# Seven quarter-block products in place of eight in the up projections of the two gated layers

## The reference

```python
D_MODEL = 1024
SEQ = 512
D_FF = 2816

def swiglu(x, w_in, w_out):
    gate, up = jnp.split(x @ w_in, 2, axis=-1)
    return (jax.nn.silu(gate) * up) @ w_out

h = h + 0.5 * swiglu(rmsnorm(h, ffn1_norm[l]), ffn1_w_in[l], ffn1_w_out[l])
h = h + hybrid_mixer(rmsnorm(h, mix_norm[l]), ...)
h = h + 0.5 * swiglu(rmsnorm(h, ffn2_norm[l]), ffn2_w_in[l], ffn2_w_out[l])
```

## Time and profile before

| | |
|---|---|
| median of 3 runs | 2323.24 us |
| profiled execution, whole | 2322.17 us |
| its span, first to last instruction | 2320.4 us |
| TensorE busy | 2283.2 us (98%), 13952 matmuls |
| TensorE weight loads busy | 1889.1 us (81%) |
| VectorE busy | 1155.9 us (50%) |
| ScalarE busy | 913.2 us (39%) |
| GpSimd busy | 1149.5 us (50%) |
| mean granted TensorE clock | 0.994 |

### The profile page before, as it was taken

How to read it: one execution, slowest core, us unless ns; L and a number is a source line. 1 busy time by engine, 2 the same in 40 slices (tenths; PEclk the granted TensorE clock), 3 DMA queues, 4 the chain that set the end, 5 groups by cost and what they waited for, 6 DMA issues and landing times.

```text
span 2320.4 us, 36943 instructions
## 1 busy us (share of the span) xinstructions
PE 2283.2 (98%) x13952; PEld 1889.1 (81%) x13952; DVE 1155.9 (50%) x1772; ACT 913.2 (39%) x1456; POOL 1149.5 (50%) x687
## 2 busy tenths in 40 slices
PE   8999999999999999999999999999999989999998
PEld 7888887889988888877777778888888878888887
DVE  5442146268743431377545466614626986731732
ACT  5332225467753321255644274212234535222222
POOL 5444444544465554444555354444445973544442
PEclk9999999999999999999999999999999989999999
DMA  4232233320033322331111113223222232332231
GB/s 167 99 99 92 99 99 102 122 69 1 10 100 100 98 93 98 98 120 64 47 34 53 43 56 104 93 97 99 93 97 84 92 100 82 100 99 99 91 99 55
DMA packets 56126, 200.09 MB, mean 86 GB/s; under 512 B 6224, under 2 KB 6480, under 8 KB 56016
## 3 DMA queue, kind: packets, MB, share of 16 engines
q1 hardware_dynamic: 54432, 195.82, 25.7%
q10 hardware_dynamic: 1584, 2.75, 0.4%
HBM read 196.45 MB, written 2.10 MB: 86 GB/s over the span
## 4 chain that ended last, share of the span: by engine, by line
PE 44%; POOL 4%; issue 3%; DVE 2%; ACT 1%; POOLq 0%; DVEq 0%; ACTq 0%
PE ps L133 13%; PE ps L135 13%; PE ps L134 13%; POOL sb_w_lo L114 2%; POOL sb_caway L3060 1%; PE ps L647 1%; PE ps L2068 0%; DVE ps L3111 0%; PE ps L661 0%; POOL sb_cu_lo L3072 0%; POOL sb_cout L3066 0%; PE ps L2064 0%; PE ps L2115 0%; PE ps L2044 0%; PE ps L2013 0%
## 5 line engine op out<-in xcount | busy, mean ns | idle before, releaser
L114 POOL TENSOR_TENSOR sb_w_lo<-sb_w_raw,sb_w_hi 128x1024 fp32r<-128x1024 f32 (+1 forms) x361 | 887.1, 2460 | 929.9 <-ACT sb_w_hi L101 928.4
L133 PE MATMUL ps<-sb_xn_hi,sb_w_hi 128*128 128x512 f32 x1688 | 669.5, 397 | 6.2 <-POOL sb_w_lo L114 3.2
L134 PE MATMUL ps<-sb_xn_lo,sb_w_hi 128*128 128x512 f32 x1688 | 657.9, 390 | 0.0
L135 PE MATMUL ps<-sb_xn_hi,sb_w_lo 128*128 128x512 f32 x1688 | 657.9, 390 | 0.0
L101 ACT ACTIVATE sb_w_hi<-sb_w_raw 128x1024 fp32r<-128x1024 f32 x362 | 379.8, 1055 | 484.1 <-PE ps L135 458.1
L133 PEld LDWEIGHTS ps<-sb_xn_hi,sb_w_hi 128*128 128x128 f32 x1688 | 316.6, 188 | 78.5 <-POOL sb_w_lo L114 4.0
L135 PEld LDWEIGHTS ps<-sb_xn_hi,sb_w_lo 128*128 128x128 f32 x1688 | 316.5, 188 | 67.2
L134 PEld LDWEIGHTS ps<-sb_xn_lo,sb_w_hi 128*128 128x128 f32 x1688 | 316.6, 188 | 65.9 <-issue 2.2
L133 PE MATMUL ps<-sb_hid_hi,sb_w_hi 128*128 128x512 f32 x864 | 336.4, 389 | 2.0 <-DVE sb_hid_lo L401 2.0
L135 PE MATMUL ps<-sb_hid_hi,sb_w_lo 128*128 128x512 f32 x864 | 336.1, 389 | 0.0
L134 PE MATMUL ps<-sb_hid_lo,sb_w_hi 128*128 128x512 f32 x864 | 336.1, 389 | 0.0
(11 more groups left out here) (491 smaller groups left out, 2957.1 us busy)
## 6 DMA issues: line engine op xcount, KB each, us to landing
sb_w_raw<-weights SPq DMA_DIRECT2D x365, 512.0 KB, 3.4
sb_stage<-x SPq DMA_DIRECT2D x4, 512.0 KB, 4.7
out<-sb_out_stage SPq DMA_DIRECT2D x8, 256.0 KB, 2.9
sb_abias<-table ACTq DMA_DIRECT2D x4, 256.0 KB, 5.4
sb_lora_w<-lora ACTq DMA_DIRECT2D x2, 256.0 KB, 2.8
sb_rstd<-table ACTq DMA_DIRECT2D x1, 256.0 KB, 2.7
sb_root<-table ACTq DMA_DIRECT2D x1, 256.0 KB, 3.0
sb_ss<-table ACTq DMA_DIRECT2D x1, 256.0 KB, 3.4
```

What stands on the lines that cost most here:

```text
L114: pool.tensor_tensor(c.w_lo[:, slot, 0:width], c.w_raw[:, slot, 0:width], c.w_hi[:, slot, 0:width].bitcast(F32), ALU.subtract).then_inc(c. ...
L133: pe.matmul(out, hi, rhs_hi(k0 + k), start=first, stop=False)
L134: pe.matmul(out, hi, rhs_lo(k0 + k), start=False, stop=False)
L135: mm = pe.matmul(out, lo, rhs_hi(k0 + k), start=False, stop=last)
```

## The change

In 38 of the 44 pairs of the gated layers (pairs 2 to 15 of each `upA`, pairs 1 to 5 of each `upB`), the gate tile and the up tile are no longer computed as two units of 8 k-tiles x 512 tokens. The pair is treated as a 2 x 2 block matrix times a 2 x 2 block matrix: the weights are A11, A12 (gate columns, lower and upper half of the 1024 features), A21, A22 (up columns), each 4 k-tiles; the activations are two feature halves by two token halves of 256. Winograd's form of Strassen's method then needs seven products of quarter blocks: each is 4 k-tiles x 3 passes = 12 matmuls of 256 columns, so a pair is 84 matmuls of 256 columns in place of 48 of 512.

What it takes around the products:

- Four weight sums for each pair, S1 = A21+A22, S2 = S1-A11, S3 = A11-A21, S4 = A12-S2 (`block_sum`, VectorE, 128x512 each, read from `w_raw`), each split into hi (`block_high`, ScalarE) and lo (`block_low`, VectorE).
- Four activation sums T1 to T4, once for each layer (`fold_x_dve`, `fold_x_act`), for four k-tiles; they are made before pair 0 is evacuated.
- Seven additions of products in PSUM, in six instructions for each pair (`fold_adds`, VectorE), and one copy (`fold_copy`, ScalarE).
- The high part of the hidden tile moves from VectorE (L399 before) to ScalarE (`parts` in `fold_up_act`).
- GpSimd splits only the gate unit (128x1024) and A22 (128x512), and the gate unit only once VectorE has finished the pair's four sums.
- The loops of these stages are written out. `c.gate` now lies in `c.y`. Some semaphores are shared to make room for new ones.

The core of the diff. TensorE:

```diff
+def fold_up_pe(pe, c, phase, xn_ready, first, i):
...
+    def folded(p):
...
+        pe.wait_ge(c.s_lo, p.u + 1)
+        pe.wait_ge(c.s_evac, p.u + START - 2)
+        block_products(pe, c, p1, p.first.spots[0], *x_part(0, 0), True, True).then_inc(c.s_used, 1)
+        block_products(pe, c, p2, p.first.spots[1], *x_part(HALF_K, 0), True, True).then_inc(c.s_used, 1)
+        pe.wait_ge(c.s_block_lo, phase.t.low + 2 * HALF_K)
+        pe.wait_ge(c.s_block_lo, p.low["S2"])
+        block_products(pe, c, p6, p.spot["S2"], *t_part(2), True, True).then_inc(c.s_used, 1)
+        pe.wait_ge(c.s_block_lo, p.low["S1"])
+        block_products(pe, c, p5, p.spot["S1"], *t_part(0), True, True).then_inc(c.s_used, 1)
+        pe.wait_ge(c.s_block_lo, p.low["S3"])
+        block_products(pe, c, p7, p.spot["S3"], *t_part(1), True, True).then_inc(c.s_used, 1)
+        pe.wait_ge(c.s_block_lo, p.low["S4"])
+        block_products(pe, c, p3, p.spot["S4"], *x_part(HALF_K, HALF_T), True, True).then_inc(c.s_used, 1)
+        pe.wait_ge(c.s_lo, p.u + 2)
+        block_products(pe, c, p4, p.spot["A22"], *t_part(3), True, True).then_inc(c.s_pe, 2)
...
+            if p.j == 1 and phase.prepared:
+                pe.wait_ge(c.s_rs, i + 1)
```

ScalarE's and VectorE's order in a pair (`after` is the next pair):

```diff
+def fold_up_act(act, c, phase, gated, hid_base, i):
...
+    for j, p in enumerate(pairs):
+        after = pairs[j + 1] if j + 1 < len(pairs) else None
+        if p.folded:
+            block_high(act, c, p, "A22")
+        if j > 0:
+            parts(pairs[j - 1])
+        if p.folded:
+            fold_copy(act, c, phase, p)
+        unit_high(act, c, after.first if after is not None else phase.following[0])
+        if after is not None and after.folded:
+            block_high(act, c, after, "S2")
+            block_high(act, c, after, "S1")
...
+        if j == 0 and phase.prepared:
+            fold_x_act(act, c, phase, i)
+        activations(p)
+        if after is not None and after.folded:
+            block_high(act, c, after, "S3")
+            block_high(act, c, after, "S4")
...
+def fold_up_dve(dve, c, phase, gated, hid_base, gain, i):
...
+        if j > 0:
+            hidden(pairs[j - 1])
+        if j > 0:
+            low(pairs[j - 1])
+        if j == 0 and phase.prepared:
+            fold_x_dve(dve, c, phase, gain, i)
+        if after is not None:
+            block_sum(dve, c, after, "S1")
+            block_sum(dve, c, after, "S2")
+            block_sum(dve, c, after, "S3")
+        if p.folded:
+            fold_adds(dve, c, p, 0)
+        if after is not None:
+            block_low(dve, c, after, "S2")
+            block_low(dve, c, after, "S1")
+            block_sum(dve, c, after, "S4")
+        if p.folded:
+            fold_adds(dve, c, p, 1)
+            fold_adds(dve, c, p, 2)
+        if gated:
+            gate = result(c, phase, p, 0)
...
+            dve.tensor_tensor(gate, gate, shaped(p, c.rs[:]), ALU.mult).then_inc(c.s_gated, 1)
+        if after is not None:
+            block_low(dve, c, after, "S3")
+            block_low(dve, c, after, "S4")
...
```

The additions, the waits of ScalarE's copies on TensorE, and GpSimd's part:

```diff
+def fold_adds(dve, c, p, n):
...
+    if n == 0:
+        dve.wait_ge(c.s_copied, p.copied)
+        dve.wait_ge(c.s_used, p.used["S2"])
+        dve.tensor_tensor(right, p6, left, ALU.add).then_inc(c.s_add, 1)
+        dve.tensor_tensor(p2, p2, left, ALU.add).then_inc(c.s_add, 1)
+    elif n == 1:
+        dve.wait_ge(c.s_used, p.used["S3"])
+        dve.wait_ge(c.s_add, p.add + 2)
+        dve.tensor_tensor(left, p7, right, ALU.add).then_inc(c.s_add, 1)
+        dve.tensor_tensor(right, p5, right, ALU.add).then_inc(c.s_add, 1)
+        dve.wait_ge(c.s_add, p.add + 3)
+        dve.tensor_tensor(p5, p5, left, ALU.add).then_inc(c.s_add, 1)
+    else:
+        both = c.ps[:, folded_banks(p.j)[1]]
+        dve.wait_ge(c.s_pe, p.u + START + 2)
+        dve.wait_ge(c.s_add, p.add + 5)
+        dve.tensor_tensor(both, both, c.ss[:], ALU.add).then_inc(c.s_add, 1)
...
+def fold_low(pool, c, phase, between=None):
...
+        if p.folded:
+            low = c.lo_blocks[:, p.spot["A22"]]
+            pool.wait_ge(c.s_hi, p.u + 2)
+            pool.tensor_tensor(low, c.w_raw[:, (p.u + 1) % RING, HALF_K:], c.hi_blocks[:, p.spot["A22"]].bitcast(F32),
+                               ALU.subtract).then_inc(c.s_lo, 1)
+        if after is not None:
+            if after.folded:
+                pool.wait_ge(c.s_sums, after.sums + 4)
+            unit_low(pool, c, after.first)
```

The activation sums, for each of four k-tiles (t1, t3 lie in `rstd`, t2, t4 in `ss`):

```diff
+        dve.tensor_scalar(product, c.x[:, k], gain(k), None, ALU.mult).then_inc(c.s_sums, 1)
...
+        dve.tensor_tensor(t1, product[:, HALF_T:], product[:, 0:HALF_T], ALU.subtract).then_inc(c.s_sums, 1)
+        dve.scalar_tensor_tensor(out=t3, in0=other[:, HALF_T:], scalar=g, in1=product[:, HALF_T:], op0=ALU.mult,
+                                 op1=ALU.subtract).then_inc(c.s_sums, 1)
...
+        dve.scalar_tensor_tensor(out=t2, in0=other[:, HALF_T:], scalar=g, in1=t1, op0=ALU.mult,
...
+        dve.scalar_tensor_tensor(out=t4, in0=other[:, 0:HALF_T], scalar=g, in1=t2, op0=ALU.mult,
...
+        for x, source in enumerate((c.rstd, c.ss)):
...
+            dve.tensor_tensor(c.t_lo[:, 2 * x:2 * x + 2, k], halves(source[:]),
+                              c.t_hi[:, 2 * x:2 * x + 2, k].bitcast(F32), ALU.subtract).then_inc(c.s_block_lo, 1)
```

405 lines of the change are left out of this document (368 added, 37 removed).

## The result

The changed kernel takes 2399.68 us (median of 4, 2396.01 to 2400.82) against 2322.31 us (2321.2 to 2323.85): 1.0329 times as long, 95% interval 1.0316 to 1.0342. The forecast was 2376 us, range 2350 to 2424: the side and the mechanism of the steady pair hold, and 24 us are missing in its sum. The profiled execution has a span of 2397.7 us, 77.3 more than before, and a mean granted clock of 0.979 in place of 0.994.

The account below looks back on a forecast made before the run. TensorE, 98% busy, bounds the kernel; once folded, it and VectorE wait by turns. Pairs 19.0, starts 28.3, constants 2 and clock 3.4 add 52.7 to 2322.17: 2374.9 profiled, 2376 us median; range 2350 to 2424, the forecast's own 2352 to 2400.

Parts of the forecast that it names:

- the steady pair: Folded pairs: VectorE and TensorE wait for each other by turns, 11.56 us a pair against 10.88, TensorE idle 1.65.
- the two starts: Start of each upA: pair 2 waits for activation sums and what follows, +13.9 and +14.4 us, together +28.3.
- the lock case: Rival: GpSimd's A22 split holds VectorE's SBUF instructions in each pair, +1.27 us a pair, 48 in all, 2424 us; 14%.
- TensorE's gain: Folded pair: 84 matmuls at 0.118 us take 9.91, 0.97 less than 10.88; at most 36.9 us for 38 pairs.
- The bounds, 26 to 35: Starts of upA: range in us for both together, from activation-sum rounds of 3.0 to 5.1 us each.
- Constants: Second upA: GpSimd's first constants follow its long split and reach into VectorE's low S3, +2 us.
- The clock: Behind each upA start: part of the time at half clock, 1.7 us each, +3.4 in all, from 0 to 8.
- the small idle of each pair I cost at nothing: Folded pairs: TensorE's short idle times cause no charged clock loss; half clock through a whole pair would be 10 us.
- The last one comes as late as it did, since L401 was held up there: Down stages: the last hidden tile comes 4.4 us behind TensorE, as before, so no cost.
- The first folded pairs: Early folded pairs are cheaper, their work not yet behind; upB's five pairs end at 56.0 us against 54.4, +1.6.
- GpSimd in VectorE's way: Folded pairs: GpSimd's splits fall beside VectorE's PSUM work or waits, so none is charged; one fits by 0.1 us.
- The signs: Profile after: matmuls at 0.118 us, 1.6 idle a pair, GpSimd's low part releasing, VectorE over 85% in upA, 13 us gaps.

Follow-up runs that it names:

- v4: v3 with folding from pair 5 in place of 4 in the two upA stages: 2307.31 us, ratio 0.993.
- The first experiment: Changed kernel with ScalarE making the high parts of S3 and S4 ahead of SiLU: 2366.25 us, ratio 1.0188.
- the second: Changed kernel with GpSimd splitting only 128 of the gate unit's 1024 columns in folded pairs, other low parts left out: 2374.8 us, ratio 1.0234.
- the padding kernel: Kernel before with only the padding tile in front of the stage buffers cut to 224 bytes from 416: 2328.83 us, ratio 1.0025.
- the fill: Changed kernel with idle matmuls of 256 columns on TensorE where it waits longest in upA and upB: 2389.19 us, ratio 1.0283.
- v3: v2 with GpSimd splitting the down stage's third unit behind upB only after VectorE's last low part of the hidden tile: 2313.9 us, ratio 0.9964.
- v1: Changed kernel folding upA from pair 4, S1 to S4 and A22 high parts ahead of SiLU, own S4 buffer, VectorE reordered, A22 split later: 2325.46 us.
- v2: v1 with unit copies earlier before plain pairs, activation sums spread over pairs 0 to 2, padding 160 bytes in place of 224: 2319.7 us.

## Why the prediction came out as it did

The side, the two chains that take turns and the two starts came nearly as computed. The total, 2399.68 us, is only just inside the forecast's own range (2352 to 2400), and the wider one reached 2424 for the lock case, which did not come as priced. That the range held is partly luck: half clock cost more than the 0 to 8 us allowed for it, and the down stages were put at nothing.

- *TensorE's gain*, 0.97 us a pair: 10.88 - 84 x 0.120 = 0.80. The rows of attention had five distances; 0.002 us on each of 84 is 0.17 a pair. v4 collects it. (The 0.2256 for 512 columns counts matmuls cut at the ends of its window; 48 at 0.2267 are the 10.88, with no loop's turn.)
- *The steady pair*, 11.56 us with TensorE and VectorE in turns, TensorE idle 1.65: measured 11.745 and 1.4. The way from L677 to S4 was 10.62 in place of 10.39 (L797 follows L677 after 0.80, not 0.72, and S4 follows L615 after 0.78), the way back 12.87 in place of 12.73, nearly all of it spacing. The first experiment put its 11.09 where this arithmetic has it. VectorE's own chain, said to be 0.14 shorter, is as long (11.73), which the second showed. 38 pairs at 0.185 more are 7.0 us.
- *The starts*, +28.3: 13.94 + 14.12 = 28.1 measured. A round took 3.64 and not 3.44, the chain behind it 10.32 and not 10.05, 1.1 us in all, and `rs` came 1.2 us later than the forecast had it. This does not show in the 13.94, since pair 1, from which it counts, came 2.3 us later itself: luck for this term. The bounds, 26 to 35, count the four rounds of one layer; for eight they are 24.8 to 41.6. Of these 2.3 us in front of pair 1, 0.8 is its wait for `rs`, which the change put there. Another 1.1 is in the padding kernel too, otherwise the kernel before (26.70 there); it has half clock at 14 us, as the changed kernel has, and before's execution has none.
- *Constants*, +2: upA took 1.9 us more in the second layer than in the first, but its slow stretches alone cost 5.8 us against 4.1. In v4, which has none in either, the difference is 3.4. So the 2 is of the right size and the 1.9 does not prove it; no run takes the constants away alone.
- *The clock*, +3.4, and "the small idle of each pair I cost at nothing": this is the step that failed, a term of the right kind and far too small. It holds for waits of 1.4 us. But the first turns have waits of 2.35 and 3.07 us, and behind most of those the clock falls. Those of 2.35 feed themselves: the next pair comes late, VectorE waits for it and hands on a late gate unit, and TensorE has the next long wait; with the fill the first upA has no such turns. Those of 3.07 in upB do not: no slow stretch stands in front of them, and the second folded pair takes 13.31 us, 13.35 with the fill. They stood in the forecast's own schedule, where the second pair takes 12.65 us (10.45 to 23.1), 2.7 of them idle, and nothing was charged for the clock behind. The fill took back 13.1 us in the folded stages: 9.7 more than charged. The Trainium skill, "TensorE: Matmul & The Clock Gate", "HAM oscillation — how this bites in real kernels", has this shape, a wait that recurs and drops the clock each time; the trace agrees in kind, with 1.5 to 2.7 us behind waits of 2.35 to 3.1, but not each time: behind two of those of 2.35 the clock stayed. I had named half clock through a pair and set it aside because I saw no row like it in before. There was one, in the second block, a wait of 3.09 us and half clock from 1.15 us behind it on:

```profile
1061.46 0.39 PE L628 MATMUL ps<-sb_ak_hi,sb_aq 128*128 128x256 f32 x1 [3.09 <-DVE sb_aq L1024]
...
1062.60:1069.40 6.80, 5.69 (x16) 4.31 (x15) 5.62 (x22) 5.70 (x17) 2.63 (x3) 0.50 0.23 77
```

- *"The last one comes as late as it did, since L401 was held up there"*: wrong by 1.7 and 3.3 us. L767 comes later than L401 did, GpSimd holds it all the same (2.30 us), and the second time the clock falls behind the wait. v3 shows the cure.
- *The first folded pairs*, +1.6 for an upB: 5.6 and 6.8. Without slow stretches (the fill) it is 2.9 in both; 0.9 of this is spacing.
- *GpSimd in VectorE's way*, nothing charged: right for the steady pairs, not for the first ones and beside the constants, where twelve instructions are held 6.0 us in all. How much of it reached TensorE no run shows.
- *The signs*: spacing, idle time, releaser and both gaps came as announced; VectorE in `upA` is busy for 80% (9.46 of 11.76 us in a steady pair), not over 85%.

Together: 7.0 longer pairs, 9.7 half clock, 5.0 downB, 0.4 in the stretches in front of pair 1 and outside the gated layers, and -0.2 at the starts make 21.9 of the 24.6 us between the sum (52.7) and the traces (77.3). 2.7 us stay open, in the early turns of upA and upB, where the held instructions are.

## What to carry to other kernels

An engine that ends every wait of the bottleneck need not be the one to shorten: cut it alone, then the other chain alone, then both. Work added to a second engine is paid by its order more than by its sum: 8.9 us of VectorE's instructions made a pair of 11.7, and the same ones in another order a pair of 10.08. Price a wait of TensorE that recurs, from some 1.7 us up, with the slow stretch that may follow.

## What the runs showed of the hardware

- **The address of a matmul's moving operand** sets 2 ns of its spacing: 192 bytes of padding moved 512-column matmuls with the hidden tile from 0.2267 to 0.2289 us, 6 us in the program. Matmuls with the activation sums went the other way in v1, 36 in 4.24 us against 4.32. Which addresses are good isn't settled: v2's, the same as before's modulo 256 bytes, are as before's.
- **The spacing of these matmuls** is 13 ns over columns / 2.4 GHz at either size (0.2267 and 0.2133; 0.120 and 0.1067). The Trainium skill's 2.5 ns ("TensorE: Matmul & The Clock Gate", "Back-to-back issue gap") doesn't hold here; the section gives it for a matmul by itself, and here each matmul loads weights of its own.
- **The clock** fell behind two of the changed kernel's four waits of 2.35 us in front of a pair and behind all five of 2.8 to 3.1 us. Over the gated layers of all fourteen traces (a fall in a wait's last microsecond counted too): behind none of 88 waits of 1.25 to 1.66 us, 2 of 4 of 1.73 and 1.74 us, 24 of 44 of 2.15 to 2.74 us, 12 of 14 of 2.8 to 3.3 us, and all 12 longer ones. Equal waits went either way, so the length of the wait alone does not decide it: in v2 the clock fell behind 3.25 us in the first layer and stayed behind 3.28 in the second:

```profile
712.16 0.39 PE L488 MATMUL ps<-sb_xn_hi,sb_w_hi 128*128 128x256 f32 x1 [3.28 <-POOL sb_w_lo L479]
```
